# Row-halved state product in a gated-linear-attention layer: two heads on the two halves of TensorE's rows, outputs in two PSUM banks

## What is computed

```
inter = einsum('bhld,bhde->bhle', qi, S)          # query times state, contraction over 64 key channels per head
A     = einsum('bhld,bhmd->bhlm', qi, ki) * causal
intra = einsum('bhlm,bhme->bhle', A, vi)
S_new = exp(be)[..., None] * S + einsum('bhld,bhle->bhde', ko, vi)
o     = inter + intra
o_gla = rmsnorm(o, gla_norm_g) * silu(gg)
```

## Time and profile before

| | |
|---|---|
| median of three runs | 1624.46 us |
| the profiled execution's own time | 1623.61 us |
| its span, first to last instruction | 1621.9 us |
| outside the span | 1.7 us |
| mean granted TensorE clock over the span | 0.982 of full speed |
| PE busy (matmul) | 1555.8 us, 96% of the span |
| VectorE, ScalarE, GpSimd busy | 58%, 37%, 34% |
| one step of the loop, read from equal instructions of two steps | 45.3 us |

### The profile page before, as it was taken

The page is one execution under the profiler, slowest core; times in us unless marked ns, Lnnn a source line. Parts: engine busy times, 40 slices in busy tenths (PEclk is TensorE's granted clock), DMA queues, the critical chain, the costliest instruction groups (busy, mean ns, idle before and its releaser), DMA issues.

```text
span 1621.9 us, 30679 instructions
## 1 busy us (share of the span) xinstructions
PE 1555.8 (96%) x11969; PEld 901.3 (56%) x11969; DVE 934.3 (58%) x1691; ACT 593.9 (37%) x1814; POOL 543.5 (34%) x567
## 2 busy tenths in 40 slices
PE   8866999999999999999999999999999999999995
PEld 3433555556656665555665666555566566655552
DVE  1674755665555656566555565656655556565752
ACT  0452433433343333333334433333333343333331
POOL 0033333334433433333443343333344334332221
PEclk9988999999999999999999999999999999999997
DMA  8934333333332332333333233233333323334122
GB/s 277 311 105 104 83 81 76 85 78 88 88 87 63 76 88 65 72 86 76 88 88 88 65 74 87 68 68 88 75 88 88 88 67 74 86 71 81 42 63 55
DMA packets 307800, 144.96 MB, mean 89 GB/s; under 512 B 269181, under 2 KB 294230, under 8 KB 307766
## 3 DMA queue, kind: packets, MB, share of 16 engines
q1 hardware_dynamic: 307766, 144.50, 37.0%
HBM read 63.12 MB, written 17.56 MB: 50 GB/s over the span
## 4 chain that ended last, share of the span: by engine, by line
PE 85%; DVE 2%; SPq 2%; DMA 1%; issue 1%; ACT 0%; POOL 0%; POOLq 0%; ACTq 0%
PE bank L457 54%; PE pairP L457 21%; PE pairQ L562 2%; PE pairQ L638 2%; PE pairQ L566 2%; PE pairQ L599 2%; PE pairQ L607 1%; PE bank L620 1%; DMA hT<-pair_tok 1%; DMA late<-pair_tok 1%; PE bank L648 1%; PE bank L644 0%; PE bank L649 0%; DVE wo_lo L923 0%; SPq L354 0%
## 5 line engine op out<-in xcount | busy, mean ns | idle before, releaser
L457 PE MATMUL bank<-w_hi,hT 128*128 128x512 f16 (+1 forms) x2640 | 741.7, 361 | 28.5 <-ACT v_tok L832 17.5
L457 PE MATMUL bank<-w_lo,hT 128*128 128x512 f16 (+1 forms) x1320 | 476.0, 361 | 0.0
L457 PEld LDWEIGHTS bank<-w_hi,hT 128*128 128x128 f16 x2640 | 259.3, 98 | 288.4 <-issue 22.6
L457 PE MATMUL pairP<-wo_hi,late 128*128 128x512 f16 x1056 | 321.4, 381 | 2.8 <-DMA late<-pair_tok 1.6
L457 PE MATMUL pairP<-wo_lo,late 128*128 128x512 f16 x528 | 201.0, 381 | 0.0
L457 PEld LDWEIGHTS bank<-w_lo,hT 128*128 128x128 f16 x1320 | 129.7, 98 | 119.8 <-issue 3.1
L457 PE MATMUL bank<-hT,w_hi 128*128 128x128 f16 x2112 | 182.0, 220 | 6.5 <-DVE k_tok L1154 3.3
L457 PE MATMUL bank<-hT,w_lo 128*128 128x128 f16 x1056 | 180.1, 220 | 0.0
L457 PEld LDWEIGHTS pairP<-wo_hi,late 128*128 128x128 f16 x1056 | 103.8, 98 | 128.4 <-ACT stage L746 2.7
L457 PEld LDWEIGHTS bank<-hT,w_hi 128*128 128x128 f16 x2112 | 164.7, 98 | 14.7 <-issue 7.4
L1288 POOL TENSOR_TENSOR gates<-gates,rden 128x512 f32<-128x512 f32 x33 | 35.2, 1067 | 336.6 <-DVE rden L1175 336.6
(11 more groups left out here) (207 smaller groups left out, 2282.5 us busy)
## 6 DMA issues: line engine op xcount, KB each, us to landing
x_in<-in_x_prompt SPq DMA_DIRECT2D x32, 512.0 KB, 3.5
x_res<-in_x_prompt SPq DMA_DIRECT2D x32, 512.0 KB, 4.1
out<-stage SPq DMA_DIRECT2D x32, 512.0 KB, 2.9
w_hi<-in_w_ada SPq DMA_DIRECT2D x5, 1024.0 KB, 9.4
w_lo<-in_w_ada SPq DMA_DIRECT2D x5, 1024.0 KB, 13.3
wo_lo<-in_w_in SPq DMA_DIRECT2D x5, 1024.0 KB, 11.9
wo_hi<-in_w_in SPq DMA_DIRECT2D x3, 1024.0 KB, 12.4
late<-pair_tok SPq DMA_TRANSPOSE x165, 3.2
```

The lines of the kernel that those rows point to most:

```text
L457: last = pe.matmul(out, a(c, i), b(c, j), start=(c == 0 and n == 0), stop=(c == KC - 1 and n == 2))
```

## The change

The 128-row state product over a pair of heads (256 output columns) becomes two products of 64 rows, one for each head (128 output columns), which read only the half of `q_int` and S that belongs to the head. The output moves: heads with q = 0 go to bank 0 of `pairQ`, heads with q = 1 to bank 1, pair b at columns 128b. `pv_ps` moves to columns 256 to 511 of both banks, one key/value head in each. As bank 0 and bank 1 now both hold parts of `o_ps` until VectorE has read it, the update of the state (`u_ps`, still columns 0 to 255 of bank 0) with its wait for `mix_gla` stands before the attention output, and VectorE's own wait for `u_mm` after L1051 is gone. The reads of L779, L1027 and L1051 follow the new places.

```diff
-        o_ps = pairQ[:, 0:512]
-        pv_ps = pairQ[:, 512:1024]
+        o_ps = pairQ[:, :].rearrange("p (q b k) -> p q b k", q=2, b=4)[:, :, 0:2, :]
+        pv_ps = pairQ[:, :].rearrange("p (g c) -> p g c", g=2)[:, :, 256:512]
...
                     for b in range(2):
-                        pe.matmul(o_ps[:, 2 * b * DV:2 * (b + 1) * DV], q_int[:, b, :], S[:, b, :, :],
-                                  start=True, stop=False)
+                        for q in range(2):
+                            r = slice(DK * q, DK * (q + 1))
+                            pe.matmul(o_ps[:, q, b, :], q_int[r, b, :], S[r, b, q, :], start=True, stop=False)
                         for q in range(2):
                             o = slice((2 * b + q) * DV, (2 * b + q + 1) * DV)
-                            last = pe.matmul(o_ps[:, o], aT[:, b, q, :], v_tok[:, o], start=False, stop=(q == 1))
+                            last = pe.matmul(o_ps[:, q, b, :], aT[:, b, q, :], v_tok[:, o], start=False, stop=True)
...
                 if c.prev:
+                    n = DEC_SEQ if c.after else P
+                    pe.wait_ge(sem["mix_gla"], t)
+                    for hd in range(GH):
+                        b, q = hd // 2, hd % 2
+                        last = pe.matmul(u_ps[DK * q:DK * (q + 1), b, :], k_tok[0:n, b, DK * q:DK * (q + 1)],
+                                         v_tok[0:n, hd * DV:(hd + 1) * DV], start=True, stop=True)
+                    last.then_inc(sem["u_mm"], 1)
                     pe.wait_ge(sem["probs_dma"], 32 * t)
                     pe.wait_ge(sem["v_keys"], t)
...
-                                    last = pe.matmul(pv_ps[:, k * HD:(k + 1) * HD], pair_ch[:, i, k, :],
+                                    last = pe.matmul(pv_ps[:, g, (k % 4) * HD:(k % 4 + 1) * HD], pair_ch[:, i, k, :],
                                                      v[:, j, HD * g:HD * (g + 1)], start=(n == 0), stop=(n == 2))
                     last.then_inc(sem["pv_mm"], 1)
-
-                    n = DEC_SEQ if c.after else P
-                    pe.wait_ge(sem["mix_gla"], t)
-                    for hd in range(GH):
-                        b, q = hd // 2, hd % 2
-                        last = pe.matmul(u_ps[DK * q:DK * (q + 1), b, :], k_tok[0:n, b, DK * q:DK * (q + 1)],
-                                         v_tok[0:n, hd * DV:(hd + 1) * DV], start=True, stop=True)
-                    last.then_inc(sem["u_mm"], 1)
...
-                        last = act.activation(junk[:, hd * DV:(hd + 1) * DV], o_ps[:, hd * DV:(hd + 1) * DV], ACT.Square,
+                        last = act.activation(junk[:, hd * DV:(hd + 1) * DV], o_ps[:, hd % 2, hd // 2, :], ACT.Square,
...
-                        last = dve.scalar_tensor_tensor(gates[:, o], o_ps[:, o], o_r[:, hd:hd + 1], gates[:, o],
+                        last = dve.scalar_tensor_tensor(gates[:, o], o_ps[:, hd % 2, hd // 2, :], o_r[:, hd:hd + 1], gates[:, o],
...
-                    dve.tensor_tensor(gates[:, 512:1024], pv_ps, gates[:, 512:1024], ALU.mult)\
-                       .then_inc(sem["mix_swa"], 1)
-                    dve.wait_ge(sem["u_mm"], t)
+                    swa = gates[:, 512:1024].rearrange("p (g c) -> p g c", g=KVH)
+                    dve.tensor_tensor(swa, pv_ps, swa, ALU.mult).then_inc(sem["mix_swa"], 1)
```

## The result

The changed kernel takes 1631.39 us (median of 7 runs, 1629.27 to 1632.76) against 1625.01 us for the kernel before (7 runs): ratio 1.0044, 95% interval 1.0034 to 1.0053. By the medians it is slower by 6.4 us, and the interval is 5.5 to 8.6 us; forecast were 8.1.

A forecast was written before the change was run, and what follows sets the result against it. PE bounds the kernel: +0.33 - 0.10 = +0.23 us per step, +7.1 over 31 steps, plus 0.95 in the last step, +8.1 us; forecast 1632.5 us, own range 1628 to 1638, 8-in-10 range 1621 to 1642.

The forecast's parts named there:

- The bound: PE, never waiting in steps t = 2 to 32, sets the time; each change per step counts 31 times.
- The boundary at 0.10 us: On PE, each change between full and partial array loses 0.10 us, bounds 0.09 and 0.11.
- The load at 0.105 us: A 128-column fp32 weight load right after a tile change exposes about 0.105 us, bounds 0.05 and 0.19.
- +0.33 us: GLA output per step: 2.14 us after the change against 1.81 before.
- Rival (B): GLA output boundaries: fp32 weights load during the drain, so not slower; 1626 or 1619.5 us; chance 0.18.
- The overlap: GLA output: a pair's two row halves run fully side by side, 0.22 us where one product cost 0.44.
- (C): Two 64-row, 128-column fp32 tiles do not run side by side; 0.44 us per step more, 1646; chance 0.12.
- (A): Row halves overlap and tile changes cost nothing; GLA output 0.44 us shorter per step, 1609; chance 0.08.
- The order at -0.10 us: State update before attention output: three tile changes instead of four, saving 0.10 us per step, bounds 0 and 0.20.
- The last step at +0.95 us: Last step: the state update waits for `mix_gla` first, delaying L599 and L1051; +0.95 us, bounds 0 and 1.3.
- The sum: Whole kernel: 7.1 us from 31 steps plus 0.95 from the last step, +8.1 us.
- 0.44 us saved, 0.82 paid, 0.10 given back: Per step: passes side by side save 0.44, four changes with loads cost 0.82, the new order saves 0.10.

## Why the prediction was right

**The bound.** PE alone sets the step: +0.22 us in its instructions is +0.22 us in the step, and no new wait appeared in the loop. One reading was wrong: the prediction says that nothing is waited for in the steps t = 2 to 32, but the step t = 2 holds the wait of 1.6 us shown above, and it gave nothing to the sum. (The run with every head by itself has no such wait, and its step t = 2 is as long as the others, 46.43 us.) The steps t = 2 to 32 together took +6.1 us where +7.1 had been summed.

**The boundary at 0.10 us.** The prediction speaks of six boundaries read; its text reads five, at 0.09 to 0.11 us. In the changed kernel the first is 825.48 - (825.33 + 0.056) = 0.09 us. With the load, 0.20 us per boundary in the section of heads by themselves, against 0.205 in the sum.

**The load at 0.105 us.** No row of before had it, and the sum of two rows was taken over bounds of 0.05 and 0.19. Measured: 0.10 in both directions. With it the term "+0.33 us" became 0.32. That the sum of two rows came out within 0.01 us is in part luck; its lower bound, 0.05, would have meant almost no change in time. Rival (B), a load hidden in the drain, falls.

**The overlap.** Full, as taken; the run with both heads on one half puts the price of (C) at 0.44 us per step and 1644.5 us, as worked out (1646). (A), boundaries that cost nothing, falls with the same rows.

**The order at -0.10 us.** -0.09 in the changed kernel, -0.10 alone.

**The last step at +0.95 us.** Here the size was off in the profiled execution: VectorE's read came 2.0 us later, not 0.95. The mechanism was the one named, with `mix_gla` ahead of the DMA. The surplus of 1.05 us is the clock. Two rows of busy time by stretch, first the changed kernel, then the kernel with the order alone (granted clock third from the end):

```profile
1594.90:1597.40 2.50, 2.46 (x32) 2.02 (x32) 0.00 (x0) 0.00 (x0) 0.56 (x1) 0.50 0.46 179
```

```profile
1584.90:1586.30 1.40, 1.40 (x32) 1.14 (x32) 0.00 (x0) 0.00 (x0) 0.86 (x1) 1.00 0.00 0
```

The same 32 passes at 1.2 GHz and at 2.4 GHz. L596's section took 1595.99 - 1594.94 = 1.05 us where it took 0.59 with the clock full, and the 24 products of L607 with their result 1.50 instead of 0.91, together 1.05 us, after PE had waited 2.96 us. The same wait left the clock full in the run of the order alone, so this part comes and goes; without it the read came 0.96 us later, as summed. The kernel before falls to 1.2 GHz as well, but only after its attention output: its granted clock is 1.00 from 1587 to 1588 and 0.50 from 1590 to 1595. Some of the microsecond is given back, as the output projection that ends the kernel then took 12.16 us in the chain of work instead of 12.73 in the run of the order alone.

**The sum.** 8.1 us said, 6.4 measured. The 31 steps gave 6.1 us instead of 7.1: 0.6 of the missing microsecond is a step of +0.21 instead of +0.23, 0.4 is the step t = 2. How the last step and the loading phase share the rest is not resolved, since the loading phase alone moves an execution by some microseconds. In the profiled execution the two errors have opposite signs, -1.0 us in the loop and +0.5 in the last step (1.4 against 0.95), so the sum is nearer than its terms.

The size that a reader should note is how close the two sides were: 0.44 us saved, 0.82 paid, 0.10 given back.

## What to carry to other kernels

On a matmul queue that is always full, count the boundaries before the rows: here each change of the part of the array in use cost 0.10 us, and 0.10 more where fp32 weights of 128 columns had to be loaded behind it, so splitting a product onto row halves pays only if the work done side by side between two boundaries saves more than that; four products of 64 rows by 128 columns in fp32 just broke even. Padding small products with zeros up to the full array, where PE sits between full-array work anyway, was worth 0.3 us per step here. When two rows bound a cost and none shows it, add up what each row says of the mechanism and keep the bounds for the range.

## What the runs showed of the hardware

- A change between full array and row tiles, between full array and column tiles, and from 32-column to 64-column tiles costs 0.09 to 0.11 us each, at 2.4 GHz. The Trainium skill (TensorEngine Tiling (Array Packing), Key Properties) says that a change of the tiling mode drains TensorE; the runs agree, with these 0.09 to 0.11 us.
- The time of the two row halves did not depend on issue order (0.65 us for eight passes, pair by pair or half by half).
- Not expected: after the same wait of 2.96 us in the last step PE went on at 2.4 GHz in one execution and at 1.2 GHz in another, with the six 64-column products of one group in 0.35 or 0.50 us. What decides it is open.
